# Packed gate rows, 64x64 products on all four quarters of TensorE, and projections moved from the gated delta recurrence into the inversion, in a two-layer hybrid decoder on one Trainium2 core

## What is computed

```
# group B, per head, in chunks of 64 tokens (8 chunks, one after the other)
g_cum = cumsum(g)                       # gates
lower = strict(k_beta @ k.T * decay)    # 64x64 per chunk and head
u, w  = solve(I + lower, v_beta), solve(I + lower, k_beta * exp(g_cum))
def step(S, ...):
    v_new = u_c - w_c @ S
    o     = (q_c * exp(g_c)) @ S + a_c @ v_new
    S     = S * exp(g_last) + (k_c * ...).T @ v_new
o = rms_norm(o) * silu(z)
# group A: sel = top_k(score, 128), for each of the 512 queries
```

## Time and profile before

| | |
|---|---|
| median of 3 executions | 2122.44 us (2121.34 to 2124.18) |
| the profiled execution | 2125.28 us, of it 2123.5 us span |
| PE busy | 2098.3 us, 99% |
| DVE busy | 1038.3 us, 49% |
| ACT busy | 775.3 us, 37% |
| POOL busy | 394.2 us, 19% |
| PE's share of the chain that ended last | 88% |

### The profile page before, as it was taken

The page is one execution under the profiler, slowest core; times in us unless marked ns, Lnnn a source line. Parts: engine busy times, 40 slices in busy tenths (PEclk is TensorE's granted clock), DMA queues, the critical chain, the costliest instruction groups (busy, mean ns, idle before and its releaser), DMA issues.

```text
span 2123.5 us, 31907 instructions
## 1 busy us (share of the span) xinstructions
PE 2098.3 (99%) x13097; PEld 1687.5 (79%) x13097; DVE 1038.3 (49%) x1427; ACT 775.3 (37%) x1096; POOL 394.2 (19%) x373
## 2 busy tenths in 40 slices
PE   9999999999999999999999999999999999999999
PEld 7888888877776888888888888887777668888887
DVE  5433333678766543333333433336887665444322
ACT  5222222474546422222232222224745563222211
POOL 1110011105035501101111110121050355111000
PEclk9999999999999999999999999999999999999999
DMA  5222222321111222222222222232212112222232
GB/s 193 88 95 99 94 95 90 139 80 62 45 69 39 100 99 99 99 86 98 94 99 99 99 99 92 92 115 100 98 43 91 42 41 100 98 88 92 95 107 75
DMA packets 30646, 192.41 MB, mean 91 GB/s; under 512 B 3216, under 2 KB 5392, under 8 KB 11984
## 3 DMA queue, kind: packets, MB, share of 16 engines
q1 hardware_dynamic: 30160, 189.80, 25.7%
q10 hardware_dynamic: 384, 1.14, 0.1%
HBM read 188.70 MB, written 2.10 MB: 90 GB/s over the span
## 4 chain that ended last, share of the span: by engine, by line
PE 88%; DVE 7%; ACT 3%; issue 1%; POOL 0%; DMA 0%; DVEq 0%; ACTq 0%
PE psum L927 27%; PE psum L929 26%; PE psum L928 26%; PE psum L1353 1%; PE psum L1364 1%; DVE wl L1806 1%; PE psum L1328 1%; PE psum L1241 1%; PE psum L1238 1%; DVE acc L1889 1%; ACT wh L1432 1%; DVE XL L1821 1%; DVE gkT L1920 0%; PE psum L1061 0%; DVE cv L1952 0%
## 5 line engine op out<-in xcount | busy, mean ns | idle before, releaser
L927 PE MATMUL psum<-XH,wh 128*128 128x512 f32 x1904 | 757.1, 398 | 4.1 <-DVE XL L1766 1.8
L929 PE MATMUL psum<-XH,wl 128*128 128x512 f32 x1904 | 743.1, 390 | 0.0
L928 PE MATMUL psum<-XL,wh 128*128 128x512 f32 x1904 | 742.6, 390 | 0.0
L927 PEld LDWEIGHTS psum<-XH,wh 128*128 128x128 f32 x1904 | 357.9, 188 | 101.4 <-issue 22.5
L929 PEld LDWEIGHTS psum<-XH,wl 128*128 128x128 f32 x1904 | 357.7, 188 | 75.6
L928 PEld LDWEIGHTS psum<-XL,wh 128*128 128x128 f32 x1904 | 358.1, 188 | 71.5 <-issue 1.0
L1814 DVE TENSOR_TENSOR wl<-raw,wh 128x2048 fp32r<-128x2048 f32 x88 | 201.7, 2292 | 159.4 <-ACT wh L1437 159.4
L928 PE MATMUL psum<-HL,wh 128*128 128x512 f32 x704 | 274.0, 389 | 0.0
L929 PE MATMUL psum<-HH,wl 128*128 128x512 f32 x704 | 274.0, 389 | 0.0
L927 PE MATMUL psum<-HH,wh 128*128 128x512 f32 x704 | 274.0, 389 | 0.0
L1432 ACT ACTIVATE wh<-raw 128x2048 fp32r<-128x2048 f32 (+1 forms) x84 | 157.2, 1871 | 304.5 <-PE psum L929 304.5
(11 more groups left out here) (256 smaller groups left out, 1971.6 us busy)
## 6 DMA issues: line engine op xcount, KB each, us to landing
raw<-weights SPq DMA_DIRECT2D x143, 1024.0 KB, 4.8
raw<-weights SPq DMA_DIRECT2D x32, 896.0 KB, 4.5
xT<-xt SPq DMA_DIRECT2D x4, 512.0 KB, 6.5
memT<-memt SPq DMA_DIRECT2D x2, 1024.0 KB, 4.7
out<-xT SPq DMA_DIRECT2D x8, 256.0 KB, 6.1
stripsA<-strip_table SPq DMA_DIRECT2D x2, 768.0 KB, 7.0
raw<-weights SPq DMA_DIRECT2D x2, 512.0 KB, 6.7
stripsB<-strip_table SPq DMA_DIRECT2D x2, 512.0 KB, 7.2
```

Of the source, the lines that this page charges most:

```text
L927: pe.matmul(out_ap, a_hi, b_hi, start=first, stop=False)
L928: pe.matmul(out_ap, a_hi, b_lo, start=False, stop=False)
L929: return pe.matmul(out_ap, a_lo, b_hi, start=False, stop=last)
```

## The change

Five edits, all in the mixer, the same in both layers:

1. `gate5` writes the gates repeated, `gate6` transposes 66 columns in place of 6, so that each pair of heads has its row pair at partitions 0, 32 and 64 of `rowg`; the three products of `rows` read 2 rows each from three different 32-row groups. `gate6` and `gate7` each stand one projection later in the list.
2. The products of the recurrence are dealt out so that neighbours use different quarters of the array: the output from the state is done half in `r1` and half in the following `r2`, the values of coming chunks are spread over the `r2` steps, and output rows of the two heads of a pair change places (the weights of `gz` and of the output projection are permuted before the launch). A new semaphore `es_ps` makes the AT products wait for the state's part.
3. `pull` in the late inversion takes 2.35 in place of 1.66; in the recurrence 0.52 in place of 0.92, and only after `u` and `r1`.
4. A round of the selection in the recurrence is in two parts, `top` after `r1` and `drop` after `r2`.
5. The mask of a block is made by one instruction in place of two. `sum` stands before the second `r1` of a block.

```diff
 RECURRENCE = [("u",)]
 for _b in range(NB):
-    RECURRENCE += [("r1", _b, 0), ("r2", _b, 0), ("r1", _b, 1)]
+    RECURRENCE += [("r1", _b, 0), ("r2", _b, 0)]
     if _b:
         RECURRENCE += [("sum", _b - 1)]
-    RECURRENCE += [("r2", _b, 1)]
+    RECURRENCE += [("r1", _b, 1), ("r2", _b, 1)]
     if _b:
         RECURRENCE += [("out", _b - 1)]
     RECURRENCE += [("oc", _b)]
 
 
-FILLED = [s for s in RECURRENCE if s[0] in ("u", "r1", "oc") or s[0] == "r2" and s[2] == 0]
+FILLED = [s for s in RECURRENCE if s[0] in ("u", "r1")]
...
-    early = [["smt"], ["mem3", "gate1"], ["gate3"], ["mem5"], [], ["gate4"], ["gate6"], [], []]
-    late = [[], ["mem4", "gate2"], [("idx", 0)], [("idx", 1)], [], [("idx", 2), "gate5"], [("idx", 3), "gate7"],
-            ["silu_qk"], []]
+    early = [["smt"], ["mem3", "gate1"], ["gate3"], ["mem5"], [], ["gate4"], [], ["gate6"], []]
+    late = [[], ["mem4", "gate2"], [("idx", 0)], [("idx", 1)], [], [("idx", 2), "gate5"], [("idx", 3)],
+            ["gate7", "silu_qk"], []]
...
-            pull(1.66)
+            pull(2.35)
         if i == 0:
             put(("vt", 2), ("vt", 3))
     for step in RECURRENCE:
         order.append(step)
         if step[0] == "r1":
-            sel(1)
+            put(("top",) + rounds[0])
+        if step[0] == "r2":
+            put(("drop",) + rounds.pop(0))
         if step in FILLED:
-            pull(0.92)
+            pull(0.52)
...
-                                mm = pe.transpose(bank[2][0:H_B, b * P:(b + 1) * P], gcum[:, b, :], const("ident"))
+                                mm = pe.transpose(bank[2][0:GROWS, b * P:(b + 1) * P],
+                                                  gcum[:, b].rearrange("p i h -> p (i h)")[:, 0:GROWS], const("ident"))
...
-                                pe.matmul(bank[4 + pair][:, :], const("pairsel")[0:H_B, pair * P:(pair + 1) * P],
-                                          rowg[:, :], start=True, stop=True).then_inc(S["eg_ps"], 1)
+                                r = slice(32 * pair, 32 * pair + 2)
+                                pe.matmul(bank[4 + pair][:, :], const("pairsel")[r, pair * P:(pair + 1) * P],
+                                          rowg[r, :], start=True, stop=True).then_inc(S["eg_ps"], 1)
...
-                            values(0).then_inc(S["vp_ps"], 1)
+                            for pair in range(3):
+                                for par in range(2):
+                                    for ch in range(2):
+                                        mm = value(0, ch, par, pair)
+                            mm.then_inc(S["vp_ps"], 1)
...
-                                for hh, par, pair, h in heads:
-                                    c0, t0 = pair * P + ch * DH, b * P + ch * DH
-                                    pe.matmul(bank[6][rows[par], c0:c0 + DH], St[rows[par], pair, :],
-                                              EGr[rows[par], pair, t0:t0 + DH], start=(pair == 0), stop=False,
-                                              skip_group_check=True)
-                                for hh, par, pair, h in heads:
-                                    mm = pe.matmul(bank[4 + par][rows[ch], pair * DH:(pair + 1) * DH],
-                                                   WT[rows[par], b, pair, ch * DH:(ch + 1) * DH], St[rows[par], pair, :],
-                                                   start=False, stop=True, skip_group_check=True)
+                                for pair in range(3):
+                                    for par in range(2):
+                                        mm = pe.matmul(bank[4 + par][rows[ch], pair * DH:(pair + 1) * DH],
+                                                       WT[rows[par], b, pair, ch * DH:(ch + 1) * DH],
+                                                       St[rows[par], pair, :], start=False, stop=True,
+                                                       skip_group_check=True)
+                                        if par == 0:
+                                            state_out(b, ch, ch, pair)
                                 mm.then_inc(S["vp_ps"], 1)
+                                if c == 2 * NB - 1:
+                                    for pair in range(3):
+                                        mm = state_out(b, ch, 1 - ch, pair)
+                                    mm.then_inc(S["es_ps"], 1)
                         elif kind == "r2":
                             b, ch = at_
                             c = 2 * b + ch
+                            beside = None if ch == 0 and b == 0 else (b + ch, 1 - ch) if b + ch < NB else None
                             pe.wait_ge(S["vn_done"], of("vn_done", c + 1))
+                            for pair in range(3):
+                                if 0 < c < 2 * NB - 1:
+                                    last = state_out(b, ch, 1 - ch, pair)
+                                if c < 2 * NB - 1:
+                                    for par in range(2):
+                                        mm = pe.matmul(bank[7][rows[par], pair * DH:(pair + 1) * DH],
+                                                       kdc[rows[ch], b, (2 * pair + par) * DH:(2 * pair + par + 1) * DH],
+                                                       U[rows[ch], b % 2, 2 * pair + par, :], start=True, stop=True)
+                                if beside:
+                                    value(*beside, 0, pair)
                             if c < 2 * NB - 1:
-                                for hh, par, pair, h in heads:
-                                    mm = pe.matmul(bank[7][rows[par], pair * DH:(pair + 1) * DH],
-                                                   kdc[rows[ch], b, h * DH:(h + 1) * DH], U[rows[ch], b % 2, h, :],
-                                                   start=True, stop=True)
                                 mm.then_inc(S["s_ps"], 1)
-                            if ch and b + 1 < NB:
-                                values(b + 1)
-                            for hh, par, pair, h in heads:
-                                c0 = pair * P + ch * DH
-                                mm = pe.matmul(bank[6][rows[par], c0:c0 + DH], U[rows[ch], b % 2, h, :],
-                                               AT[rows[ch], b, hh, :], start=(c == 0 and pair == 0), stop=True, skip_group_check=True)
+                            if 0 < c < 2 * NB - 1:
+                                last.then_inc(S["es_ps"], 1)
+                            for pair in range(3):
+                                if beside:
+                                    value(*beside, 1, pair)
+                                for par in (ch, 1 - ch):
+                                    if c and pair == 0 and par != ch:
+                                        pe.wait_ge(S["es_ps"], of("es_ps", c))
+                                    c0 = pair * P + ch * DH
+                                    mm = pe.matmul(bank[6][rows[1 - par], c0:c0 + DH], U[rows[ch], b % 2, 2 * pair + par, :],
+                                                   AT[rows[ch], b, 3 * par + pair, :], start=(c == 0 and pair == 0),
+                                                   stop=True, skip_group_check=True)
                             mm.then_inc(S["o_ps"], 1)
...
+                    def value(b, ch, par, pair):
+
+                        return pe.matmul(bank[4 + par][rows[ch], pair * DH:(pair + 1) * DH],
+                                         XTF[rows[ch], b, 3 * slot_of(par, ch, LEVELS) + pair, :],
+                                         gvN[rows[ch], b, (2 * pair + par) * DH:(2 * pair + par + 1) * DH],
+                                         start=(pair == 0), stop=(b + ch == 0), skip_group_check=True)
...
+                    def state_out(b, ch, par, pair):
+
+                        c0, t0 = pair * P + ch * DH, b * P + ch * DH
+                        return pe.matmul(bank[6][rows[1 - par], c0:c0 + DH], St[rows[par], pair, :],
+                                         EGr[rows[par], pair, t0:t0 + DH], start=(pair == 0), stop=False,
+                                         skip_group_check=True)
...
-                            chain.step(dve.tensor_tensor(unsel[b][:, :], wrk[:, 0:w], acc[b][:, :], ALU.is_equal))
-                            chain.join()
-                            dve.tensor_scalar(unsel[b][:, :], unsel[b][:, :], NEG, None, ALU.mult
+                            dve.tensor_scalar(unsel[b][:, :], wrk[:, 0:w], GONE, NEG, ALU.is_gt, ALU.mult
```

More of the change, by code:

```diff
@@ L646, in hybrid_trunk @@
         XTF = sb("XTF", [P, NB, H_B, DH])
+        with ExitStack() as first:
+            sb("behind_DT", [P, 2, H_B, DH], F32, first)
+            gcum = sb("gcum", [P, NB, P // H_B, H_B], F32, first)
         with ExitStack() as early:
@@ L1304, in gdn @@
                                       start=True, stop=True).then_inc(S["os_ps"], 1)
-                    def values(b):
-                        for hh, par, pair, h in heads:
```

(37 more changed lines are left out.)

15 lines of the change are left out of this document (8 added, 7 removed).

## The result

The changed kernel takes 2131.86 us (median of 5, 2127.12 to 2133.30), the one before 2122.44 us in the same comparison (2121.32 to 2126.11): the ratio is 1.0037, 95% interval 1.0023 to 1.0052. It is slower, by 9.4 us in the median. In the four later comparisons the kernel before has medians of 2124.0 to 2124.7 us, and beside those the changed kernel is 7 to 8 us slower. The profiled execution took 2132.87 us; the forecast for it was 2128.

What follows compares the result with a forecast made beforehand. TensorE, 88% of the chain that ended last, was taken to bound the kernel. Per layer -2.5 + 0.5 + 3.65 + 0.15 - 0.4 = +1.4 us, +2.8 in all: 2125 us, own range 2120 to 2130, widest 2115 to 2133.

Steps and rivals of the forecast that it cites:

- the likeliest case: Whole kernel: the summed forecast, +1.4 us a layer, +2.8 in all, median 2125 us; given 42%.
- the clock: Rival, 18%: new pauses make TensorE's granted clock fall; two more falls a layer give +5 us, 2130.
- a stall that is absorbed: Rival, 20%: the TensorE wait before the inversion's last `w` is not there or is absorbed; -7.3 us, 2118.
- a block of 6 us: Rival, 12%: a recurrence block takes 6 us, not 7; -6.5 us over two layers, about 2118.5.
- neighbours that do not overlap: Rival, 8%: small products on the same rows do not overlap, 33 ns a record; eight blocks grow by 10 us, 2135.
- the last of its own signs: Forecast is wrong if the clock row shows falls in the recurrence that were not there before.
- Rows: Gate rows before the first `decay`: three products near 1.1 us, not 2.84, and a shorter mask; -2.5 us a layer.
- The later gate steps: `gate7` comes right ahead of the activation chain TensorE waits for at L1069; +0.5 us a layer, bounds 0 and +0.6.
- The stall: Before the inversion's last `w`, TensorE waits for unit 15 from DVE: +3.65 us a layer, bounds 2.5 to 4.5.
- The pace of the small products: Recurrence: one record per quarter in some 62 ns; 0.37 us a piece, 1.1 us a chunk against some 2.
- The recurrence itself: Four blocks, 7.0 us between starts, 27.65 us, plus 13.1 us moved ahead, against 40.6: +0.15 us a layer, bounds ±2.5.
- The mask: Attention, third block: one DVE instruction less reaches TensorE only in part; -0.4 us a layer, bounds 0 and -0.8.

Runs made afterwards that it cites:

- without the stall: Changed kernel with both halves of unit 15's split directly behind the last `n` on DVE, and its one eighth behind the last `w`: 2119.80 us, ratio 0.9979.
- The filled stall: Changed kernel with 18 products of 384 columns, of no use to the result, on TensorE while it waits for `wl`: 2128.42 us, ratio 1.0016.
- the earlier `out`: `out` ahead of the second `St` on DVE: 2112.63 us with unit 15's split moved earlier, 2109.96 in the changed kernel with the old placing of projections.

## Why the prediction was right, and where it fell short

The direction of the likeliest case held, and so did the widest range, 2115 to 2133, by 1.1 us. The forecast's own range from its bounds, 2120 to 2130, did not, and the outcome given the most weight, the same within 0.2% (0.42), did not come; slower had 0.35. Of the four rivals one came, the clock; a stall that is absorbed, a block of 6 us and neighbours that do not overlap did not. The point was 6.9 us too low in the median, 4.9 in the profiled execution: a change of 2.8 us was forecast, and the two profiled executions are 7.6 apart. By the last of its own signs, falls of the clock in the recurrence that were not there before, the forecast counts as wrong in this step.

*Rows* were forecast at -2.5 us with the shorter mask in it. The products were sized right (1.13 us), and the kernels with packed rows and the joined mask but without the move show the term itself: 23.5 us in place of 25.9, -2.4. In the changed kernel it is -1.7 and -3.3. The eighth of `dk` that the move puts ahead of the first `n` takes 0.7 of it back, and 1.6 of the second is a fall of the clock that only the kernel before had there.

*The later gate steps* cost the +0.5 that was forecast: 0.5 in the second layer here and in the pairs of kernels.

*The stall* was forecast at 3.65 and is 3.41 us, behind the instructions that were named. That a term read off the list of steps held this well is the best part of the working.

*The pace of the small products* was forecast at 0.37 us for 18 records on three quarters. The rival in which neighbours on the same rows do not overlap is refuted. One `r1` begins at 588.62 and its last product at 588.97, the other groups are alike. Here the trace of before was a better guide than the rule of the Trainium skill in "TensorE: Matmul & The Clock Gate", Part 3, The mechanism, which is about weight loads and different row groups.

*The recurrence itself* was forecast at 27.65 us and takes 28.75 in the undisturbed layer, counted as the forecast counted, to the start of the last `sum` (581.36 to 610.11; the table counts on to the second record of `sum`). The first three blocks take 7.25, not 7.0 us, and the last 7.0, not 6.65. This is the term of +0.15, mis-sized by 1.1 a layer. Against it, the moved work weighs less than the 13.1 us summed up: 0.7 us stands ahead of the first `n`, and without the stall, but with the move, the stage from the first `n` to `u` is 11.6 and 11.5 us longer than without the move, 12.3 together. Why 0.8 us less, was not looked into. The two errors nearly cancel, which is luck. "The 8 us saved in small products become waits" had the mechanism right in the main, and the size wrong: where TensorE bounds, the saving is about 3.5 us a layer (2.1 net and 1.4 of waits). And not all of what the other edits save is lost with the move, since without the cover they shorten the recurrence from 32.4 to 29.2 us.

*The mask* in the attention was forecast at -0.4 and gives -0.7 to -0.8.

*What failed* is the sum's silence on the clock. The text put it apart as a rival with 18%, at 2130, and priced two more falls a layer. The profiled execution has four more in its mixers, one in the first layer and three in the second, and 10.2 us at the lower clock made the second layer's recurrence 4.2 us longer than the first's (33.4 against 29.2). That is most of the 4.9 us that are missing; the falls behind the stall (1.4 and 1.6 us) cancel against moved work that weighs less than was summed up and a fall of before that went. The forecast should have had falls in the likeliest case, for the terms it did contain, a pause of 3.65 us and one of 1.7 in each block, are what the falls stand beside. The filled stall shows it for the long pause, the kernels without stall and with the earlier `out` make it likely for the recurrence.

Not settled is what exactly decides whether a fall comes. The two layers run the same list, and the recurrence of the second fell three times where that of the first did not once. The kernel with packed rows alone lost the fall in the attention, and nothing in that stage had been changed. And one kernel differs from itself: the one before took 2121 to 2122 us in those of its runs that had a mean clock of 1.000.

## What to carry to other kernels

Before work is moved out of a stage as it became cheaper, work out the chain that lies under it. Here projections covered 7 us of DVE and ACT steps a block. Without them a block lasts as long as these steps, and products that TensorE saves count only where they stand in that chain, while the moved projections are paid in full elsewhere. With the projections left where they were, the other edits make the kernel 12 us faster; with the move all of them together make it 7 to 9 us slower.

A pull that takes products earlier must take what feeds them earlier too; a list walked by all engines does not do that by itself. And the pause of 3.4 us was paid twice here, once as itself and once as clock (1.4 to 1.6 us), where the first layer's recurrence had three of 0.96 to 1.65 us and no fall. That of two orders with the same sum of waits the one with short ones is the better follows from this, and was not tested by itself.

## What the runs showed of the hardware

The granted clock fell to 1.2 GHz at the end of a pause of 3.4 us (574.4, the pause ending at 574.7) and in the second layer 1.3 us behind one (1632.6, the pause ending at 1631.3), and in the profiled execution with products without use in that pause it stayed up in both places. A stretch of 3.4 us at the lower level cost 1.4 to 1.6 us, where 1.7 would be half of it; that TensorE waits for part of such a stretch anyway is the likely reason, not a measured one.

The median of one kernel carries this too: the kernel before took 2121 to 2122 us when its mean clock was 1.000, and up to 2127 at 0.998. So of 12 us between two versions some 5 can be clock.

TensorE stood 1.58 us inside a run of small products in the first layer's inversion with nothing in the trace that it waited for ("issue"), 1.2 to 1.5 in the other four kernels whose projections were moved, at most 0.6 at a time in those where they were not, and never in the second layer. The cause was not looked for.
